# mLSTM decay matrix: from three accumulated matmuls to activations over broadcast row maxima, with the v and o biases added at eviction

## The reference, cut to what matters

```python
def mlstm_chunk(carry, inp):
    C, n, m = carry
    q, k, v, ig, lf = inp
    b = jnp.cumsum(lf, axis=-1)
    logD = jnp.where(causal, b[..., :, None] - b[..., None, :] + ig[..., None, :], -jnp.inf)
    inter = b + m[..., None]
    m_t = jnp.maximum(inter, jnp.max(logD, axis=-1))
    D = jnp.exp(logD - m_t[..., None])
    w_state = jnp.exp(inter - m_t)
    S = jnp.einsum('bhtd,bhsd->bhts', q, k) * D
    num = jnp.einsum('bhts,bhse->bhte', S, v) + w_state[..., None] * jnp.einsum('bhtd,bhde->bhte', q, C)
    den = jnp.sum(S, axis=-1) + w_state * jnp.einsum('bhtd,bhd->bht', q, n)
    h = num / jnp.maximum(jnp.abs(den), jnp.exp(-m_t))[..., None]
```

## Time and profile before

| | |
|---|---|
| median of 3 runs | 3501.86 us (3500.81 to 3501.96) |
| the profiled execution | 3493.6 us |
| its span, first to last instruction | 3491.8 us |
| TensorE / VectorE / ScalarE / GpSimd busy | 3017.8 / 2141.9 / 2153.4 / 1207.1 us |
| mean granted TensorE clock | 0.979 of full |
| DMA | 1187.66 MB, 340 GB/s over the span |

### The profile page before, as it was taken

The page is one execution under the profiler, slowest core; times in us unless marked ns, Lnnn a source line. Parts: engine busy times, 40 slices in busy tenths (PEclk is TensorE's granted clock), DMA queues, the critical chain, the costliest instruction groups (busy, mean ns, idle before and its releaser), DMA issues. The chain is left out here.

```text
span 3491.8 us, 41982 instructions
## 1 busy us (share of the span) xinstructions
PE 3017.8 (86%) x9327; PEld 1423.4 (41%) x9327; DVE 2141.9 (61%) x5330; ACT 2153.4 (62%) x7215; POOL 1207.1 (35%) x1119
## 2 busy tenths in 40 slices
PE   8999999978888888888888888888888888888886
PEld 2565435543433444344334433443444344334331
DVE  2232145566667666766666666667666766676665
ACT  2133113337777677777777777777777767777775
POOL 0000100023444444445444444444443444444443
PEclk9999999989999999999999999999999999999999
DMA  8300003169999999999999999999999999999998
GB/s 326 118 28 25 4 0 107 57 259 420 404 420 413 416 399 419 417 400 420 412 398 409 419 419 413 402 419 396 418 408 419 406 407 412 419 409 396 419 420 334
DMA packets 166486, 1187.66 MB, mean 340 GB/s; under 512 B 19326, under 2 KB 19454, under 8 KB 28114
## 3 DMA queue, kind: packets, MB, share of 16 engines
q0 software_dynamic: 155328, 1115.96, 78.0%
q1 hardware_dynamic: 10900, 68.95, 5.2%
HBM read 1175.59 MB, written 9.23 MB: 339 GB/s over the span
## 5 line engine op out<-in xcount | busy, mean ns | idle before, releaser
L772 PE MATMUL ps<-r_w,r_yT 128*128 128x512 f32 (+1 forms) x3168 | 1522.1, 614 | 329.6 <-ACT r_yT L1070 321.7
L1545 DVE SCALAR_TENSOR_TENSOR r_yT<-r_w,r_qk 128x1024 bf16<-128x1024 f32 x792 | 969.3, 1225 | 678.5 <-DMA r_w<-in_peer_uv,gidx 664.1
L500 POOL DMA_INDIRECT r_w<-in_peer_uv,gidx x792 | 882.3, 1114 | 999.6 <-PE ps L772 827.4
L772 PEld LDWEIGHTS ps<-r_w,r_yT 128*128 128x128 f32 (+1 forms) x3168 | 551.4, 189 | 1220.5 <-issue 1219.3
L772 PE MATMUL ps<-r_yT 128*128 128x512 f32 (+1 forms) x1056 | 516.6, 622 | 105.5 <-ACT r_yT L1070 96.0
L1062 ACT ACTIVATE mixc<-mixc 128x1 f32<-128x1 f32 x1056 | 207.3, 196 | 455.8 <-DVE r_yT L1545 450.5
L500 POOL DMA_INDIRECT r_yT<-in_peer_uv,gidx x264 | 292.6, 1108 | 548.9 <-PE ps L772 498.6
L1070 ACT ACTIVATE r_yT<-ident,mixc 128x128 f32<-128x128 f32 x1024 | 411.4, 402 | 94.3 <-ACT mixc L1066 1.2
L1066 ACT ACTIVATE mixc<-mixc 128x1 f32<-128x1 f32 x1056 | 409.1, 387 | 35.0
L1065 ACT ACTIVATE mixc<-mixc 128x1 f32<-128x1 f32 x1056 | 408.4, 387 | 33.8
L1545 DVE SCALAR_TENSOR_TENSOR r_yT<-r_yT,r_qk 128x1024 bf16<-128x1024 f32 x264 | 322.8, 1225 | 127.9 <-DMA r_yT<-in_peer_uv,gidx 110.1
(11 more groups left out here) (276 smaller groups left out, 2375.5 us busy)
## 6 DMA issues: line engine op xcount, KB each, us to landing
r_w<-in_ada_w SPq DMA_DIRECT2D x12, 2048.0 KB, 8.4
r_w<-in_peer_uv,gidx POOLq DMA_INDIRECT x792
r_w<-in_w_lin SPq DMA_DIRECT2D x16, 512.0 KB, 4.4
r_yT<-in_peer_uv,gidx POOLq DMA_INDIRECT x264
r_vo<-in_x_prompt SPq DMA_DIRECT2D x8, 512.0 KB, 18.5
r_w<-in_w_vo SPq DMA_DIRECT2D x2, 2048.0 KB, 8.2
r_w<-in_w_out SPq DMA_DIRECT2D x1, 4096.0 KB, 13.4
r_w<-in_x_prompt SPq DMA_DIRECT2D x8, 512.0 KB, 3.5
```

The costliest lines, as they stand in the source:

```text
L500: pool.indirect_dma_start(ring[place(h, j)], None, table, bass.IndirectOffsetOnAxis(gidx_t[:, h, j:j + 1], 0))\
L772: mm = nc.tensor.matmul(ps[0:r, 2 * p + c, :], diag[:, j % 4, 0:r], row[:, D + c * 512:D + (c + 1) * 512], start=h == 0 and j == 0, stop=h ...
L1545: V.scalar_tensor_tensor(udump[j % 2], ring[i][:, 0:D], 1.0, h2[:, t, :], ALU.mult, ALU.mult, accum_out=dots[:, i:i + 1]).then_inc(dot_don ...
```

## The change

The decay matrix no longer comes from TensorE. The running maxima `mro` are stored to DRAM when they are done, and loaded back as a broadcast to all 128 partitions (`top_b`, 4 × 1056 values each), queued on GpSimd behind the row transposes, because it overwrites the rows. The row a becomes a fourth column set in `colT` (36 transposes instead of 27). ScalarE computes exp(a[s] − M[t]) with four 128x128 activations per tile, the column as bias; GpSimd sets the entries of the future to zero with a select. `negm`, `offsets`, the mask and the two extra buffers of `decay` and `hh` go.

The bias products go; VectorE evicts v and o (`evict_vo`), adding the bias out of a copy broadcast to 128 partitions, and Tanh runs in place afterwards on ScalarE (`open_gate`). VectorE's row work and evictions are interleaved by hand. The row transposes (`turn_rows`) stand before the last tile's two units. The five row loads on GpSimd wait for the last eviction instead of for the columns.

```diff
-            pe.wait_ge(bvo_ld, 32)
+            def turn_rows():
+                pe.wait_ge(row_exp, 1)
+                pe.wait_ge(lg_ev, 24)
+                for t in range(NT):
+                    r = rows(t)
+                    for a, row in enumerate((wst, nmr, wkr, aro)):
+                        nc.tensor.transpose(ps[0:r, 4, (t * 4 + a) * 4:(t * 4 + a) * 4 + 4], row[:, t * P:t * P + r],
+                                            ident[0:H_B, 0:H_B])
+                nc.tensor.matmul(ps[:, 4, 160:196], ones[0:H_B, :], wcd[0:H_B], start=True, stop=True).then_inc(row_tr, 1)
+
             for t in range(NT):
                 r = rows(t)
+                if t == NT - 1:
+                    turn_rows()
                 for n, w in enumerate((wv, wo)):
                     bank = z_bank()
                     if t == 0:
                         pe.wait_ge(vo_ld[n], 16)
                     for k in range(KD):
-                        nc.tensor.matmul(ps[0:r, bank, :], hT[:, k, t * P:t * P + r], w[:, k, :], start=k == 0, stop=False)
-                    nc.tensor.matmul(ps[0:r, bank, :], ones[0:1, 0:r], bvo[n],
-                                     start=False, stop=True).then_inc(z_mm, 1)
+                        m = nc.tensor.matmul(ps[0:r, bank, :], hT[:, k, t * P:t * P + r], w[:, k, :],
+                                             start=k == 0, stop=k == KD - 1)
+                    m.then_inc(z_mm, 1)
...
-            def decays(i):
+            def turn_keys(i):
...
-                if i >= 1:
-                    pe.wait_ge(d_exp, i)
-                if i >= 3:
-                    pe.wait_ge(y_ev, i - 2)
-                pe.wait_ge(negm_ready, i + 1)
-                dst = ps[0:r, 1, :].rearrange("p (h t) -> p h t", h=H_B)[:, :, 0:r]
-                nc.tensor.matmul(dst, ident[0:r, 0:r], mask[0:r, 0:r].unsqueeze(1).broadcast_to([r, H_B, r]),
-                                 start=True, stop=False)
-                nc.tensor.matmul(dst, aro[:, cs], seleye[:, :, 0:r], start=False, stop=False)
-                nc.tensor.matmul(dst, ones[0:H_B, 0:r], negm[:, i % 2, :, 0:r], start=False, stop=True).then_inc(d_mm, 1)
...
+            def open_gate(t):
+                r = rows(t)
+                act.wait_ge(z_ev, 51 + 2 * (t + 1))
+                nc.scalar.activation(og[0:r, t, :], og[0:r, t, :], ACT.Tanh, scale=0.5).then_inc(og_t, 1)
+
+            act.wait_ge(f_abs, 1)
+            nc.scalar.activation(nmr, wst, ACT.Exp, scale=-1.0).then_inc(f_exp, 1)
             for t in range(NT):
-                evac_vo(t)
-                if t == 2:
-                    act.wait_ge(f_abs, 1)
-                    nc.scalar.activation(nmr, wst, ACT.Exp, scale=-1.0).then_inc(f_exp, 1)
-                if t == 6:
+                open_gate(t)
+                if t == 4:
...
             def decay_exp(i):
-                r = rows(ORDER[i])
-                act.wait_ge(d_mm, i + 1)
-                if i >= 2:
-                    act.wait_ge(p_ready, i - 1)
-                nc.scalar.activation(decay[i % 2][0:r, :, 0:r], ps[0:r, 1, :].rearrange("p (h t) -> p h t", h=H_B)[:, :, 0:r],
-                                     ACT.Exp).then_inc(d_exp, 1)
+                t = ORDER[i]
+                r = rows(t)
+                if i == 0:
+                    act.wait_ge(top_ld, 16)
+                    act.wait_ge(col_ready, 2)
+                if i >= 1:
+                    act.wait_ge(p_ready, i)
+                for h in range(H_B):
+                    m = nc.scalar.activation(decay[0:r, h, 0:r], top_b[0:r, h, t * P:t * P + r], ACT.Exp, scale=-1.0,
+                                             bias=colT[0:r, t, 3, h:h + 1])
+                m.then_inc(d_exp, 1)
...
+            pool.wait_ge(top_done, 1)
+            pool.dma_start(top_dram[:, :], mro).then_inc(top_st, 16)
...
-            pool.wait_ge(col_ready, 2)
+            pool.wait_ge(top_st, 16)
+            pool.wait_ge(row_tr, 1)
+            pool.dma_start(top_b, top_dram[:, :].partition_broadcast(P)).then_inc(top_ld, 16)
+
+            def cut_future(i):
+                r = rows(ORDER[i])
+                pool.wait_ge(d_exp, i + 1)
+                nc.gpsimd.affine_select(out=decay[0:r, :, 0:r], in_=decay[0:r, :, 0:r], compare_op=ALU.is_ge, fill=0.0, base=0,
+                                        pattern=[[0, H_B], [1, r]], channel_multiplier=-1).then_inc(d_cut, 1)
+
+            pool.wait_ge(z_ev, 51 + 2 * NT)
             mod_rows(a2b, 4, 1, DEC, bc_ld)
...
+            cut_future(0)
+            cut_future(1)
             pool.wait_ge(c_upd, 1)
             store_state(1, 3)
+            cut_future(2)
+            cut_future(3)
             store_x1(0)
+            cut_future(4)
...
             for i in range(1, 6):
                 store_x1(i)
+                if i + 4 < NT:
+                    cut_future(i + 4)
...
+            def evict_vo(t):
+                r = rows(t)
+                for n, dst in enumerate((vext[0:r, t, :, 0:DK], og[0:r, t, :])):
+                    u = 51 + 2 * t + n
+                    dve.wait_ge(z_mm, u + 1)
+                    z, b = ps[0:r, u % 4, :], bvo[0:r, n, :]
+                    if n == 0:
+                        z, b = (x.rearrange("p (h e) -> p h e", h=H_B) for x in (z, b))
+                    V.tensor_tensor(dst, z, b, ALU.add).then_inc(z_ev, 1)
+                link(V.memset(vext[0:r, t, :, DK:DK + 1], 1.0))
...
+            dve.wait_ge(bvo_ld, 16)
+            dve.wait_ge(z_ev, 51)
+            evict_vo(0)
             for t in range(NT):
                 c = slice(t * P, t * P + rows(t))
                 link(V.tensor_tensor_scan(wst[:, c], ones[0:H_B, 0:rows(t)], fro[:, c], 0.0, ALU.mult, ALU.add))
...
+            evict_vo(1)
...
+            evict_vo(2)
...
+            evict_vo(3)
+            for t in range(3):
+                gate_out(t)
+            evict_vo(4)
+            gate_out(3)
...
+            for t in range(5, NT):
+                evict_vo(t)
+                gate_out(t - 1)
+            gate_out(NT - 1)
             dve.wait_ge(row_tr, 1)
...
             def weights(i):
                 r = rows(ORDER[i])
                 dve.wait_ge(s_mm, i + 1)
-                dve.wait_ge(d_exp, i + 1)
+                dve.wait_ge(d_cut, i + 1)
```

More of the change, by code:

```diff
@@ L86, in build @@
         ones = sb("ones", [P, P])
-        mask = sb("mask", [P, P])
         seleye = sb("seleye", [H_B, H_B, P])
@@ L410, in _ @@
             ch = Chain(pool, pool_step)
-            for m, v in ((ident[:, :], 0.0), (mask[:, :], 0.0), (seleye[:, :, :], 0.0), (ones[:, :], 1.0), (ssq, 1.0), (ssqh, 1.0), (ssq2, 1.0)):
+            for m, v in ((ident[:, :], 0.0), (seleye[:, :, :], 0.0), (ones[:, :], 1.0), (ssq, 1.0), (ssqh, 1.0), (ssq2, 1.0)):
                 ch.link(nc.gpsimd.memset(m, v))
@@ L433, in _ @@
             pool.wait_ge(lg_mm, 24)
-            for n in range(2):
-                pool.dma_start(bvo[n], A["b_in"][:, 2048 + n * W_B:2048 + (n + 1) * W_B]).then_inc(bvo_ld, 16)
+            pool.dma_start(r_wr[:, :], A["b_in"][0, 2048:2048 + 2 * W_B].partition_broadcast(P)).then_inc(bvo_ld, 16)
             pool.wait_ge(z_ev, 51)
@@ L600, in _ @@
                     for k in range(KD):
-                        nc.tensor.matmul(ps[0:r, bank, :], hT[:, k, t * P:t * P + r], w[:, k, :], start=k == 0, stop=False)
-                    nc.tensor.matmul(ps[0:r, bank, :], ones[0:1, 0:r], bvo[n],
-                                     start=False, stop=True).then_inc(z_mm, 1)
-            pe.wait_ge(row_exp, 1)
-            pe.wait_ge(lg_ev, 24)
-            for t in range(NT):
-                r = rows(t)
-                for a, row in enumerate((wst, nmr, wkr)):
-                    nc.tensor.transpose(ps[0:r, 4, (t * 3 + a) * 4:(t * 3 + a) * 4 + 4], row[:, t * P:t * P + r],
-                                        ident[0:H_B, 0:H_B])
-            nc.tensor.matmul(ps[:, 4, 128:164], ones[0:H_B, :], wcd[0:H_B], start=True, stop=True).then_inc(row_tr, 1)
+                        m = nc.tensor.matmul(ps[0:r, bank, :], hT[:, k, t * P:t * P + r], w[:, k, :],
+                                             start=k == 0, stop=k == KD - 1)
+                    m.then_inc(z_mm, 1)
             pe.wait_ge(z_ev, 51 + 2 * NT)
             pe.wait_ge(col_ready, 2)
-            def decays(i):
+            def turn_keys(i):
                 t = ORDER[i]
-                r, cs = rows(t), slice(t * P, t * P + rows(t))
+                r = rows(t)
                 if i >= 1:
@@ L696, in project @@
                 m.then_inc(o_mm, 1)
-            decays(0)
+            turn_keys(0)
             products(0)
```

83 lines of the change are left out of this document (33 added, 50 removed).

## The result

| | before | after |
|---|---|---|
| median, taken side by side | 3501.34 us (3500.69 to 3501.96, 4 runs) | 3455.99 us (3453.14 to 3457.87, 4 runs) |
| the profiled execution | 3493.60 us | 3455.63 us |
| its span | 3491.8 us | 3453.9 us |
| first gather of the expert stage | 742.92 us | 707.42 us |

The ratio is 0.987 (95% interval 0.9853 to 0.9887): 45.4 us faster, where 36.5 were forecast. From profile to profile the gain is 3493.60 − 3455.63 = 38.0 us. The rest of this text is about those 7.4 us between the two differences.

A forecast was written before the change was run, and what follows sets the result against it. TensorE bounds the projections and mLSTM tiles, DMA gathers the expert stage. 17.7 + 0.6 + 1.2 + 0 + 2.0 + 5 × 2.99 = 36.5 us, off the 3501.86 median: 3465.4 us, range 3458 to 3480.

The forecast's parts named there:

- Step 1: v and o projection: without bias matmuls units come 6.87 us apart instead of 8.11, 22.0 us gained, all on the path.
- Step 2: v and o projection: VectorE's first eviction stands behind log(1+x), so TensorE stalls 1.8 us near 405 us; bounds 0 and 3.
- Step 3: End of the projections: 36 row transposes ahead of the last units, loop starts at 509.1 instead of 526.84, 17.7 us earlier.
- Step 4: Steady mLSTM tiles: three decay matmuls leave, 2.99 us a tile in five tiles; exponential and select cost zero, 4.3 us cover.
- Rival E: mLSTM tiles: GpSimd's select, on the path beyond 4.9 us, makes the kernel slower; at 11 us, 3514 us. Chance 0.04.
- Step 5: First mLSTM tiles, partly at half clock: gains of 0.6, 1.2, 0 and 2.0 us without the decay products.
- the lower bound: Whole gain before the expert stage: 34 us if the clock stays low throughout the first tiles.
- the upper bound: Whole gain before the expert stage: 40.6 us with full clock and without the 1.7 us dip of 618 to 624 us.
- A: Whole kernel: the forecast as summed, median 3465.4 us. Chance 0.69.
- B: The clock falls at both new pauses, behind the 405 us stall and before the loop: 31 us gained, 3471. Chance 0.12.
- C: mLSTM loop doesn't shorten, as exponential, select and weights chain in place of the decay matmuls: 3484. Chance 0.09.
- D: Expert stage takes the gain back, its gathers running no faster and starting against other traffic: 3502. Chance 0.04.

The follow-up runs named there:

- The fourteen selects: The changed kernel with the select done fourteen times over in each tile, one after the other: 3466.67 us, ratio 0.9909.
- the other profile of before: Profile of the kernel before, run again with nothing changed: 3491.9 us profiled, median 3500.85 us over 10 runs, ratio 1.0.
- the short kernel before: The kernel before without the expert stage's tiles, everything up to the routing of the first two heads kept: 783.98 us.
- its short form: The changed kernel without the expert stage's tiles, cut in the same way as the kernel before: 739.10 us.
- the decay alone: The kernel before with only broadcast maxima, select and 36 row transposes moved; biases stay matmuls, ScalarE evicts: 3477.73 us, ratio 0.9937.
- the short pauses: The changed kernel with two evictions inside log(1+x), columns copied and state cleared ahead of the last eviction: 3454.37 us, ratio 0.9876.
- the split products: The kernel before with the three decay products in the middle of the first half projection instead of ahead of it: 3496.27 us, ratio 0.9992.
- dense products in the waits: Five unused 128x512 products put into TensorE's waits of the first three steps, added to the short pauses: 3449.91 us, ratio 0.9864.
- memory places: The kernel before with the changed kernel's memory places (small DRAM tensor added, mask moved, larger column tensor), same computation: 3498.91 us, ratio 0.9997.

## Why the prediction was right, and where it was wrong

**Step 1 (bias matmuls, 22.0 us): right.** Units 6.88 us apart, forecast 6.87.

**Step 2 (stall, 1.8 us): right.** 1.82 us (its own terms, 406.7 − 405.0, give 1.7); TensorE resumed at 407.87, forecast 406.7, and the whole stage began 0.8 later than in the profile of before (378.32 instead of 377.50).

**Step 3 (rows and loop start): right.** 2.4 us for the rows (2.6), a pause of 3.62 (3.5), loop start 510.42, of which 0.8 came in with the stage: forecast 509.1. The broadcast was issued at 493.52 and landed 8.6 us later, forecast 492 and 8.2, ahead of its use.

**Step 4 (decay products, 2.99 a tile): right.** 21.68 became 18.70, 2.98. The select took 0.63 on 128x512, the value taken from the 4x512 row, and 4.26 us passed from its end to the weights (4.3). **One sentence of it was wrong**: that each microsecond beyond this would be paid per tile. The fourteen selects show 4.78 us of waiting on VectorE at no cost to the step. The cover has to be counted to TensorE's next need, the heads at 620.90: less 0.69 for the weights and with a single select ending at 608.55 + 0.63, it is 11.0 us. Rival E's point of 4.9 us was therefore too low for steady tiles; in the first four it is nearly right.

**Step 5 (first tiles): the sum near, the terms not.** The steps were 4.44, 9.34, 11.16 and 18.86, against 4.93, 8.96, 10.69 and 21.70: gains of 0.5, −0.4, −0.5 and 2.8 us, where 0.6, 1.2, 0 and 2.0 were said. The sum is 2.5 against 3.8. The low clock did reach through the first three steps, as the lower bound had it, and was gone in the fourth. Of its reason, "only small matmuls are left there, behind a 3.5 us pause", the pause alone is not enough: with 0.77 us the clock fell behind the loop's start instead of ahead of it, and the steps were no shorter (4.73, 9.34 and 11.17). Another execution of the changed kernel had 3.83, 7.23 and 10.71 with clocks of 0.72 and 0.89 there, so these terms vary by some 3 us from execution to execution.

**The sum**: 3457.1 was forecast for a profile, 3455.63 came, and two offsets helped. The steps themselves gave 526.84 − 510.42 = 16.4 at the loop's start (forecast 17.7), 2.5 in the first tiles (3.8) and 5 × 2.98 = 14.9: 33.8. The dip of the one profile adds 1.7, which makes the 35.5 us by which the first gather is earlier. The last 2.4 us are the expert stage, 2748.9 us before and 2746.5 after, about as much as it varies between executions of one kernel (2746.9 in the other profile of before).

**The base: this is the step that failed.** "The sum below is made against the profiled one and the difference is taken off the median" holds only if the median execution is the profiled one plus something that the change leaves alone. It is not. Before, the median execution carries more low-clock time in the mLSTM tiles than the profiled one did: the short kernel before, profiled in its median execution, shows it as a second step 3.67 us longer and four dips instead of one, 8.7 us in all. The changed kernel hardly has this: nine executions within 5.4 us, and a gain of 44.9 us with no expert stage at all. With 8.7 us added, 36.5 + 8.7 = 45.2, or 3501.86 − 45.2 = 3456.7; measured was 3455.99. So close a fit is luck, as the 8.7 come from one execution.

Two parts make it up, and the profiles bear them out unequally. In the steady tiles the change cuts the run of small matmuls ahead of each half projection from 6.1 to 3.1 us, and none of the kernels with the short run has a dip there. The prediction had this in its hands, as "1.7 us, which follows 6 us of small matmuls that now become 3", but put it once, into the upper bound, as a feature of this one profile; it can come once, four times or not at all. In the first tiles, step 5 took the profiled execution's 46.28 us (four steps up to the first steady tile) for the kernel's. Over the six profiles of kernels that keep the three decay products there, two of them of the kernel before itself, these steps take 46.3 to 53.6 us; over the five of the changed kernel (twice), its short form, the decay alone and the short pauses, 40.6 to 44.1. In the short kernel's execution this part is 3.67 of the 8.7 us, in that of the split products it is all there is, and the prediction had no term for it.

**The rivals.** A came true in its steps. B had the clock as a cost; behind the stall at 405 us it did not fall at all (1.00 over the stage, units of 6.88), and in the steady tiles the clock was a gain. The Trainium skill, TensorE: Matmul & The Clock Gate, section "HAM oscillation — how this bites in real kernels", lays the low clock to idle gaps between bursts. The runs agree with it where dense products in the waits kept 1.00, and in the tile before the steady ones, where the clock was low behind five of the six waits of about 3 us and behind none of the eight shorter ones. They go beyond it in the steady tiles, where the clock fell in stretches with 7.70 of 8.00 us busy. C, D and E did not occur: steps of 18.70 us, an expert stage of 3453.9 − 707.42 = 2746.5 us, and nobody waiting for the select. What came by the median, a gain above 41 us, had been given 0.02.

**What stays open.** Why one execution has four dips and another one or none, and why the executions form two groups, was not found; nor was the first tiles' part of the spread separated from the steady tiles' by a run. Splitting the run alone gave 3.8 us by medians with an interval that holds zero and left two groups, so the shares in the 7.4 us rest on profiles of single executions, and no execution of the upper group of the whole kernel before was profiled. The expert stage varies by itself, between 2744.9 us (memory places) and 2751.3 us (fourteen selects), with no cause looked for.

## What to carry to other kernels

A profile is one execution: if the median lies off it by a fifth of the expected gain, find out which events come and go between executions before the difference is carried over, by running the unchanged kernel often and by cutting off the long stage behind. A low-clock stretch seen once in a profile may come several times or not at all in another execution wherever its pattern repeats, so it belongs into the range with more than its one size. Cover is to be counted to the next need of the engine that bounds the stage, not to the next instruction that reads the result.

## What the runs showed of the hardware

- The granted clock fell with no more than 0.30 us of pause on TensorE, behind 6.1 us of matmuls that were small or had 4 input rows, but for a mask product of 1.10 us, and cost about 1.7 us in the half projection that followed (5.11 to 5.40 instead of 3.70). It came in 8 of 30 steady tiles with such a run, and in none of 40 where the run was cut short or split.
- Behind a wait of TensorE of 2.97 to 3.36 us, ahead of the first output projection, the half projection took 4.82 to 6.08 us in five of six profiles; behind 1.07 to 1.42 us it took 3.62 in all eight.
- Five unused products of 128x512 in waits that were there anyway raised the granted clock over the loop's first steps from 0.52 (508 to 520 us) to 1.00 (505 to 520 us), with one dip left at 526 us, and the median went from 3454.37 to 3449.91 us, though they are work added.
- A select of 128x512 float32 on GpSimd took 0.63 us, the same as one of 4x512; of 32x128, 0.305 us.
